# Feed-forward layers: separate semaphores for quarter loads, operand sums by copies and adding transfers, plain convolution in PSUM

## What is computed

```python
def gated_conv_ffn(x, w_gate, w_up, conv_w, conv_b, w_down):
    g = jnp.einsum('bsd,df->bsf', x, w_gate)
    g = causal_dwconv3(g, conv_w) + conv_b
    up = jnp.einsum('bsd,df->bsf', x, w_up)
    return jnp.einsum('bsf,fd->bsd', jax.nn.silu(g) * up, w_down)
```

## Time and profile before

| what | value |
|---|---|
| three runs | 1818.08, 1818.07, 1819.58 us; median 1818.08 |
| profiled execution | 1823.57 us, of it the span of the instructions 1821.9 us |
| mean granted clock of PE | 0.987 of full |
| first feed-forward layer | 873 to 1144 us of the span; its first seventh product at 922.2 |
| second feed-forward layer | 1418 to 1689 us; its first seventh product at 1466.6 |

### The profile page before, as it was taken

One profiled execution on the slowest core, in us unless ns is written; L12 is line 12 of the kernel. 1 busy time (PEld: TensorE's weight loads), 2 busy tenths in 40 slices (PEclk: granted clock), 3 DMA queues, 4 the chain that ended last, 5 costly groups with the idle time before them and its releaser, 6 DMA issues.

```text
span 1821.9 us, 29445 instructions
## 1 busy us (share of the span) xinstructions
PE 1719.3 (94%) x9907; PEld 1494.8 (82%) x9907; DVE 1126.7 (62%) x1967; ACT 892.1 (49%) x1677; POOL 649.6 (36%) x733
## 2 busy tenths in 40 slices
PE   7999999999999999999878889999999888889998
PEld 6788789999878888888678888888887678888887
DVE  6677767777743345754777777433355777877332
ACT  6676766666632233333355555323454455555222
POOL 3555666565410001001355665010013355665000
PEclk9999999999999999999999999999999999999999
DMA  4111123323233342233345554432332345554332
GB/s 132 50 50 54 50 59 83 83 70 82 70 92 92 92 144 76 70 98 94 92 103 135 125 129 111 136 99 88 93 93 81 92 100 128 138 130 108 107 95 87
DMA packets 294704, 173.58 MB, mean 95 GB/s; under 512 B 13807, under 2 KB 279922, under 8 KB 294610
## 3 DMA queue, kind: packets, MB, share of 16 engines
q1 hardware_dynamic: 281714, 148.69, 28.4%
q0 software_dynamic: 12704, 23.34, 7.3%
q10 hardware_dynamic: 192, 0.33, 0.1%
HBM read 147.02 MB, written 2.16 MB: 82 GB/s over the span
## 4 chain that ended last, share of the span: by engine, by line
PE 61%; DVE 16%; issue 8%; POOL 6%; ACT 5%; DMA 4%; DVEq 0%; ACTq 0%; POOLq 0%
PE ps L410 37%; PE ps L2559 8%; PE ps L1026 3%; DVE w_split L2620 3%; PE ps L3023 2%; DVE w_split L367 2%; PE ps L876 2%; DMA w_raw_b<-in_w_ffn_gate_dram 2%; DMA w_raw<-in_w_ffn_gate_dram 2%; POOL e_sum L2799 1%; POOL w_split L2620 1%; DVE tmp L1369 1%; PE ps L889 1%; DVE arena_r L1374 1%; PE ps L855 1%
## 5 line engine op out<-in xcount | busy, mean ns | idle before, releaser
L410 PE MATMUL ps<-arena_r,w_split 128*128 128x512 f32 x2094 | 486.3, 393 | 15.7 <-DVE w_split L367 13.9
L410 PEld LDWEIGHTS ps<-arena_r,w_split 128*128 128x128 f32 x2094 | 394.8, 189 | 104.4 <-DVE w_split L367 17.2
L410 PE MATMUL ps<-u,w_split 128*128 128x512 f32 x1641 | 400.0, 395 | 0.0
L367 DVE TENSOR_TENSOR w_split<-w_raw,w_split 128x1024 fp32r<-128x1024 f32 x149 | 188.9, 1268 | 297.1 <-ACT w_split L351 297.0
L351 ACT CAST w_split<-w_raw 128x1024 fp32r<-128x1024 f32 (+4 forms) x249 | 213.2, 874 | 300.4 <-PE ps L410 264.8
L410 PEld LDWEIGHTS ps<-u,w_split 128*128 128x128 f32 x1641 | 304.0, 188 | 62.9 <-issue 0.5
L2559 PE MATMUL ps<-xs_u,w_split 128*128 128x256 f32 x1728 | 235.8, 291 | 55.8 <-POOL w_split L2620 47.5
L2559 PEld LDWEIGHTS ps<-xs_u,w_split 128*128 128x128 f32 x1728 | 219.1, 195 | 65.3 <-DVE tmp L2915 31.6
L1977 POOL TENSOR_TENSOR tmp<-tmp 128x512 f32<-128x512 f32 x33 | 46.7, 1416 | 261.1 <-ACT tmp L1933 232.4
L365 POOL TENSOR_TENSOR w_split<-w_raw,w_split 128x256 fp32r<-128x256 f32 x168 | 123.0, 763 | 23.7 <-ACT w_split L351 23.7
L1974 POOL COPY tmp<-tmp 128x512 f32<-128x512 f32 x5 | 3.2, 649 | 349.0 <-ACT tmp L1933 183.4
(11 more groups left out here) (335 smaller groups left out, 2675.0 us busy)
## 6 DMA issues: line engine op xcount, KB each, us to landing
w_raw<-in_w_in_dram SPq DMA_DIRECT2D x118, 256.0 KB, 3.1
w_raw<-in_w_ffn_down_dram SPq DMA_DIRECT2D x64, 256.0 KB, 3.0
w_raw<-in_w_ffn_gate_dram SPq DMA_DIRECT2D x52, 256.0 KB, 3.2
w_raw<-in_w_ffn_up_dram SPq DMA_DIRECT2D x52, 256.0 KB, 3.2
w_raw_b<-in_w_ffn_up_dram SPq DMA_DIRECT2D x36, 256.0 KB, 3.2
w_raw_b<-in_w_ffn_gate_dram SPq DMA_DIRECT2D x36, 256.0 KB, 3.2
w_raw_b<-w_raw_b POOLq DMA_DIRECT2D x36, 256.0 KB, 4.3
w_raw<-w_raw POOLq DMA_DIRECT2D x36, 256.0 KB, 3.7
```

The source lines that it names most:

```text
L367: ins = eng.tensor_tensor(lo, r, hi, ALU.subtract)
L410: last = pe.matmul(out_ap, w_tile(c, ws, k - n0), moving(k, ms), start=start and n == 0, stop=stop and n == len(total) - 1, skip_group_che ...
```

## The change

- **Loads.** u1 and u2 add to a semaphore `up_load`, g1 to `g1_load`, g2 to `g2_load`, and each user waits for what it reads. The first sum waits for u1 and u2; the third sum now waits for g1.
- **Operand sums.** ACT begins the four sums by copies, with sign, of one term each (`act_x_begin`); five transfers on POOL's queue that add (`pool_x_add`, 512 KB each) complete them: T1N (one), T4 (two), T2 (one, which reads T1N), T3 (one). T4 is now begun as -B21 and gets B22 and T1N. The fifth, T3's, is issued only when T1N and T2 have landed. `pool_x` goes.
- **Plain pairs.** Their convolution, silu input and hidden rows lie in PSUM (`plain_conv`, banks 4 and 5) instead of `cnv` and `hid`. p1 of the first two pairs of the seven products waits for the low half of the plain pair that used its bank.
- **Plain units.** Units 2 to 7 all use `product_low_last`, where only unit 2 did.
- **Orders.** The written orders of ACT, DVE and POOL are changed: high and low halves of units stand earlier, POOL's first sum stands between the adding transfers.

```diff
@@ -71,6 +71,7 @@
...
 WEIGHT_OF = {"p1": "g1", "p2": "g2", "p3": "g2", "p4": "u2", "p5": "e", "p6": "g1", "p7": "u1"}
+LOADS = {"u1": "up", "u2": "up", "g1": "g1", "g2": "g2"}
 QUARTERS = ("g1", "u1", "u2", "g2")
...
@@ -245,7 +246,7 @@
...
         cnv, at = view(tmp, at, 2, SEQ)
-        hid, at = view(tmp, at, 1, SEQ)
+        at += SEQ
         rbc_ffn, at = view(tmp, at, 1, SEQ)
...
@@ -2463,8 +2464,10 @@
...
 
-        def loaded(eng, layer, i, gs):
-            eng.wait_ge(sem(f"pair_load{gs % 2}"), num(64 * (N_PAIR // 2 * layer + (gs - PLAIN) // 2 + 1), i, 128))
+        def loaded(eng, layer, i, gs, part):
+
+            per = 32 if part == "up" else 16
+            eng.wait_ge(sem(f"{part}_load{gs % 2}"), num(per * (N_PAIR // 2 * layer + (gs - PLAIN) // 2 + 1), i, 2 * per))
 
...
@@ -2504,7 +2507,7 @@
...
                 sp.dma_start(quarter(layer, gs, name).rearrange("p (k n) -> p k n", k=4), src) \
-                    .then_inc(sem(f"pair_load{gs % 2}"), 16)
+                    .then_inc(sem(f"{LOADS[name]}_load{gs % 2}"), 16)
 
...
@@ -2538,7 +2541,9 @@
...
                 out_ = bank(R_BANK + gs % 2, 0, HT)
-                if not (isinstance(i, int) and gs < PLAIN + 2):
+                if isinstance(i, int) and gs < PLAIN + 2:
+                    pe.wait_ge(sem("ffn_a_lo"), FT * layer + gs - 1)
+                else:
                     pe.wait_ge(sem("ffn_a_done"), per_tile(layer, i, gs, 2))
...
@@ -2569,19 +2574,18 @@
...
             for j in range(2 * PLAIN):
-                if j == 2:
-                    pe.wait_ge(sem("w_hi"), c0 + 3)
-                    product_low_last(pe, bank(2), c0 + 2, moving, range(KT), True, lambda: w_ready(pe, c0 + 2), True) \
-                        .then_inc(sem("w_used"), 1)
-                    continue
-                w_ready(pe, c0 + j)
-                if j < 2:
-                    pe.wait_ge(sem("h_tile"), hs_before(tag) + KT - 1 + j)
                 if j >= 4:
...
                         pe.wait_ge(sem("ffn_g_read"), PLAIN * layer + j // 2 - 1)
+                if j >= 2:
+                    pe.wait_ge(sem("w_hi"), c0 + j + 1)
+                    product_low_last(pe, bank(j % 4), c0 + j, moving, range(KT), True, lambda: w_ready(pe, c0 + j), True) \
+                        .then_inc(sem("w_used"), 1)
+                    continue
+                w_ready(pe, c0 + j)
+                pe.wait_ge(sem("h_tile"), hs_before(tag) + KT - 1 + j)
                 product(pe, bank(j % 4), c0 + j, moving, ready=h_ready(pe, tag) if j == 0 else None) \
...
@@ -2599,7 +2603,7 @@
...
             if kind in ("p1", "p2", "p4"):
-                loaded(act, layer, i, gs)
+                loaded(act, layer, i, gs, LOADS[WEIGHT_OF[kind]])
             else:
...
@@ -2624,21 +2628,30 @@
...
         X_SOURCE = {"p1": B11, "p2": B21, "p3": B22, "p4": T4, "p5": T1N, "p6": T2, "p7": T3}
-        X_SUMMED = {"p5": 1, "p6": 2, "p7": 3, "p4": 4}
+        X_SUMMED = {"p5": 1, "p6": 2, "p7": 3}
+        X_BEGUN = 4
 
...
 
-            if kind in X_SUMMED:
-                act.wait_ge(sem("x_sum"), 4 * layer + X_SUMMED[kind])
+            if kind == "p4":
+                act.wait_ge(sem("x_fourth"), 32 * layer + 32)
+            elif kind in X_SUMMED:
+                act.wait_ge(sem("x_sum"), 48 * layer + 16 * X_SUMMED[kind])
             else:
...
 
+        def act_x_begin(act, layer, m):
+
+            act.wait_ge(sem("x_dve"), X_STEPS * layer + KT)
+            dst, first, sign = ((T1N, B12, -1.0), (T4, B21, -1.0), (T2, B22, 1.0), (T3, B12, -1.0))[m]
+            act.activation(dst, first, ACT.Copy, scale=sign).then_inc(sem("x_hi"), 1)
+
         def dve_x(dve, layer, kind):
 
-            dve.wait_ge(sem("x_hi"), len(X_ORDER) * layer + X_ORDER.index(kind) + 1)
+            dve.wait_ge(sem("x_hi"), (X_BEGUN + len(X_ORDER)) * layer + X_BEGUN + X_ORDER.index(kind) + 1)
             hi, lo = XS[kind][:, :, HI, :], XS[kind][:, :, LO, :]
...
@@ -2651,14 +2664,23 @@
...
 
-        def pool_x(pool, layer, m):
-
-            pool.wait_ge(sem("x_dve"), X_STEPS * layer + KT)
-            if m in (1, 3):
-                pool.wait_ge(sem("x_sum"), 4 * layer + m)
-            dst, in0, in1, op = ((T1N, B11, B12, ALU.subtract), (T2, T1N, B22, ALU.add), (T3, B22, B12, ALU.subtract),
-                                 (T4, T2, B21, ALU.subtract))[m]
-            pool.tensor_tensor(dst, in0, in1, op).then_inc(sem("x_sum"), 1)
+        def pool_x_add(pool, layer, m):
+
+            begun = (X_BEGUN + len(X_ORDER)) * layer
+            pool.wait_ge(sem("x_hi"), begun + (1, 2, 3, 2, 4)[m])
+            if m == 2:
+                pool.wait_ge(sem("x_sum"), 48 * layer + 16)
+            elif m == 3:
+                pool.wait_ge(sem("x_sum"), 48 * layer + 16)
+                pool.wait_ge(sem("x_fourth"), 32 * layer + 16)
+            elif m == 4:
+                pool.wait_ge(sem("x_sum"), 48 * layer + 32)
+            dst, term = ((T1N, B11), (T4, B22), (T2, T1N), (T4, T1N), (T3, B22))[m]
+            pool.dma_start(dst, term, accum_op=ALU.add).then_inc(sem("x_fourth" if m in (1, 3) else "x_sum"), 16)
+
+        def plain_conv(f):
+
+            return bank(R_BANK + f % 2)
 
...
@@ -2667,20 +2689,22 @@
...
             act_stats(act, tag)
+
             def tap(f):
...
                 if f > 1:
-                    act.wait_ge(sem("ffn_a_done"), FT * layer + f - 1)
-                act.activation(cnv[:, f % 2, :], gpad[:, f % 2, 0:SEQ], ACT.Copy, scale=ffn_vec(layer, 0, f)) \
+                    act.wait_ge(sem("ffn_a_lo"), FT * layer + f - 1)
+                act.activation(plain_conv(f), gpad[:, f % 2, 0:SEQ], ACT.Copy, scale=ffn_vec(layer, 0, f)) \
                     .then_inc(sem("ffn_tap"), 1)
...
                 act.wait_ge(sem("ffn_conv"), 2 * FT * layer + 2 * f + 2)
-                act.activation(cnv[:, f % 2, :], cnv[:, f % 2, :], ACT.Silu, bias=ffn_vec(layer, 3, f)).then_inc(sem("ffn_silu"), 1)
+                act.activation(cnv[:, f % 2, :], plain_conv(f), ACT.Silu, bias=ffn_vec(layer, 3, f)) \
+                    .then_inc(sem("ffn_silu"), 1)
 
...
                 act.wait_ge(sem("ffn_a_done"), FT * layer + f + 1)
-                act.copy(a_r[:, f, HI, :], hid[:, 0, :]).then_inc(sem("ffn_a_hi"), 1)
+                act.copy(a_r[:, f, HI, :], plain_conv(f)).then_inc(sem("ffn_a_hi"), 1)
 
...
@@ -2688,29 +2712,33 @@
...
             tap(0)
+            plain_unit(3)
             silu(0)
-            plain_unit(3)
+            plain_unit(4)
+            act_x_begin(act, layer, 0)
             plain_hi(0)
-            plain_unit(4)
+            tap(1)
+            act_x_begin(act, layer, 1)
+            plain_unit(5)
+            silu(1)
+            act_x_begin(act, layer, 2)
+            act_x_begin(act, layer, 3)
             act_x(act, layer, "p1")
-            tap(1)
-            silu(1)
             act_x(act, layer, "p2")
-            plain_unit(5)
+            plain_unit(6)
+            plain_hi(1)
+            tap(2)
             act_x(act, layer, "p5")
-            plain_hi(1)
-            plain_unit(6)
-            tap(2)
             silu(2)
+            plain_unit(7)
             act_x(act, layer, "p6")
-            plain_unit(7)
+            plain_hi(2)
+            act_seventh(act, layer, 0, *ORDER[0])
             act_x(act, layer, "p7")
-            plain_hi(2)
-            act_x(act, layer, "p4")
-            act_seventh(act, layer, 0, *ORDER[0])
             tap(3)
...
             silu(3)
+            act_x(act, layer, "p4")
             act_seventh(act, layer, 0, *ORDER[2])
...
@@ -2792,7 +2820,7 @@
...
             def first_sum(i, gs):
-                loaded(pool, layer, i, gs)
+                loaded(pool, layer, i, gs, "up")
                 if not (isinstance(i, int) and gs < PLAIN + 2):
...
@@ -2800,6 +2828,7 @@
...
             def third_sum(i, gs):
+                loaded(pool, layer, i, gs, "g1")
                 pool.wait_ge(sem("summed_w"), summed_to(layer, i, gs, 1))
...
@@ -2817,14 +2846,15 @@
...
             scaled(0)
-            pool_x(pool, layer, 0)
-            pool_x(pool, layer, 1)
+            pool_x_add(pool, layer, 0)
+            pool_x_add(pool, layer, 1)
             scaled(1)
-            pool_x(pool, layer, 2)
-            pool_x(pool, layer, 3)
+            first_sum(0, PLAIN)
+            pool_x_add(pool, layer, 2)
+            pool_x_add(pool, layer, 3)
+            third_sum(0, PLAIN)
+            pool_x_add(pool, layer, 4)
             scaled(2)
-            first_sum(0, PLAIN)
-            third_sum(0, PLAIN)
             second_sum(0, PLAIN)
...
@@ -2863,44 +2893,44 @@
...
                 dve.wait_ge(sem("w_used"), c0 + 2 * f + 2)
-                if f:
-                    dve.wait_ge(sem("ffn_a_lo"), FT * layer + f)
-                dve.tensor_tensor(hid[:, 0, :], bank(2 * (f % 2) + 1), cnv[:, f % 2, :], ALU.mult).then_inc(sem("ffn_a_done"), 1)
```

(34 more changed lines are left out.)

## The result

The changed kernel takes 1794.37 us, the median of 3 runs (1793.38 to 1794.91), against 1818.08 before. The ratio is 0.9866, 95% interval 0.9844 to 0.9888: 23.7 us faster. The forecast was 1785, range 1766 to 1804. The sign and the range hold. The forecast's own case (1776 to 1795) holds by 0.6 us only, and the sum was 33.

The account below looks back on a forecast made before the run. TensorE was taken as nearly always busy, its waits mostly for GpSimd's low split in a loop through the loads. 23 us (periods) plus 10 (layer starts) gave 33 off 1818.1, so 1785, range 1766 to 1804.

Parts of the forecast that it names:

- The forecast's own case: Whole kernel: the time falls between 1776 and 1795 us, with 1785 likeliest; chance 0.49.
- Part 1: Settled periods: separate load semaphores start the first sum earlier, 0.75 us in each of 31 periods, 23 us (12 to 40).
- Rival three: Settled periods: another member of the loop holds GpSimd's round, so only 10 us are won, 1808; chance 0.11.
- Rival one: Settled periods: u2 lands as fast as g2 and takes the port first, 50 us won, 1768; chance 0.12.
- Part 2: Layer start: low-half pass last from unit 2 on, no pauses before units 3, 5, 7; plain units end 8.8 us earlier.
- Part 3: Layer start: adding transfers replace GpSimd's operand sums, p6 5.3 us earlier; after a clock loss, 10 us for two layers.
- d: Layer start: time a 512 KB adding transfer needs, taken as 6 us, between 4.9 and 8.8.
- u2 lands about 900.5: Layer start: landing time of the pair's second up load, after which GpSimd's first sum and T2's transfer follow by 902.3.
- rival four: Layer start: adding transfers held in GpSimd's queue beside full unit loads make it slower, 1830 at 17 us each; chance 0.08.
- Rival two: Layer start: its gain is eaten by slow adding transfers, only the semaphores win, 1795 or 1800; chance 0.2.
- Half a fall: Layer start: clock loss after pauses of about 3 us, set at 1.2 us and taken off the gain.
- Part 4: Layer start: plain convolution in PSUM; p1 newly waits for plain pair 2's low half, some 0.7 us, nothing else.

Follow-up runs that it names:

- e3: The changed kernel with GpSimd's wait for g1 put ahead of the first sum instead of the third; ratio 0.9842 to the kernel before.
- e1: The kernel before with the separate load semaphores and nothing else; 1800.14 us against 1820.27, ratio 0.9887.
- e2: The changed kernel with one semaphore for all four loads again; 1818.85 us, ratio 0.9991 to the kernel before.
- e11: The changed kernel with a pair's loads issued u1, u2, g1, g2 instead of u1, g1, u2, g2; ratio 0.9840 to the kernel before.
- e4: The changed kernel with GpSimd's T2 and T4 transfer issues ahead of the pair's first sum; ratio 0.9854 to the kernel before.
- e7: The changed kernel with the four operand sums computed by GpSimd again instead of adding transfers; ratio 0.9827 to the kernel before.
- e5: The changed kernel with plain pair 2's scaling ahead of GpSimd's first sum and p6's and p7's x halves later; ratio 0.9826 to the kernel before.

## Why the prediction was right, and where it was wrong

The mechanism of the periods was right and that of the starts was wrong. 1794 lies inside the range because the starts, forecast at 10 us, brought a small loss and no more, and because the periods brought somewhat more than forecast; the second of these is partly luck.

**Part 1, the semaphores: right in kind, near in number by two errors against each other.** Forecast 0.75 a period and 23 us; measured 26.8. In the settled period it was 0.52 (11.86 to 11.34: 1043.62 and 1055.48 before, 1042.14 and 1053.48 after), and 31 times that is only 16. The start of the sum came 0.75 earlier, where the prediction put it, by the split of p6, but the second wait on GpSimd took 0.26 back, which the prediction had at nothing; e3 shows that the gap is its price. The rest came from what the sum had left out. The waits of before that stand between the first pair and the layer's end, layers 1 and 2 together, are 49.1 us, those of after 30.3: 18.8 from pauses. The remaining 8.0 is clock: before had five rounds like the earlier trace rows in these two stretches, with products of up to 2.72; after has none. Not all of it hangs on the semaphores. With them alone (e1) the periods gain 19.1, and with all but them (e2) 3.3, none of it in pauses (50.3 against 49.1). The remaining 4.4 come only with both; why is not shown, and the runs of one kernel lie up to 7 us apart. Rival three (the loop holds) falls with e1. Rival one (u2 in 3.0, the port first) falls too: u2 took 3.7, and e11 shows that an earlier u2 meets DVE's split in most rounds. Its two rounds with the sum in front, at pauses of 0.24 and 0.28, are what that rival had described.

In e11 the first sum took 1.65 instead of 1.29 where DVE's split had begun 0.20 before it, and the split took 1.82 instead of 0.69 where the sum had begun 0.01 before it. By the rule of the Trainium skill (SBUF — State Buffer, Who interferes with whom), which the prediction cited, one of the two waits for the other; the rows agree.

**Part 2, plain units: right.** No pause, full clock, and 5.44 a unit instead of the 5.7 that was used. The plain units end 10.1 us earlier, from +48.80 to +38.7, where 8.8 was said.

**Part 3, the operand sums: wrong, by the loads and not by d.** Forecast: p6 5.3 earlier; measured: 0.9 later (+56.62 against +55.68). (The 19 us that it names for d = 4.9 are 17.6 by its own terms, 2 x (6.6 + 2.2).) Step by step, from the layer's start (forecast, measured): unit 7's load let go +21.07, +20.90; u2 landed +27.07, +32.1; T2 issued +28.87, +34.09; T3 landed +40.87, +46.3; p6 +50.37, +56.62. The step that failed is "u2 lands about 900.5". It allowed 6.0 us from the release for five issues and a landing, in the 0.37 and 3.8 of a settled period. It took 4.5 to reach u2's issue, with 1.45 and 1.53 for the issues of u1 and g1, and 6.7 to land. That is 5 of the 6.2 us missed; most of the rest, 0.8, is the chain from T3's landing to p6. d itself was 5.1 for T2 and 6.6 for T3, 11.7 for both where 2 x 6 was set. The prediction asked what the loads do to the adding transfers (rival four), and never what these do to the loads. e4 and e7 show that: T2 issued earlier makes u2 4.4 later; without the adding transfers u2 lands 3.8 sooner behind the release. Rival two, the start eaten, is what happened, by another route than a d near 8.8. Its number, 1795, is also nearer to the measured 1794 than the forecast is.

The Trainium skill's figure (DMA: Bandwidth & Descriptors, Anatomy of one DMA) would have made d 3.2, an estimate; the shortest here took 5.1, so the measurement decides against it. The same page (SWDGE vs HWDGE vs iDMA) says that transfers issued by GpSimd and by SP run on the same engines, and the trace agrees, with 38.8% and 67.9% of them taken at once: that rule, not weighed in the prediction, spoke against the step that failed.

**The clock in the start: too small.** Half a fall (1.2) was set. p1, p2 and the two products from p6 on took 2.90, 2.93 and 4.62, 4.2 more than at full clock. Part of it hides in the waits of p2 and p6; the 1.6 behind p6 cannot.

**Part 4, the new wait of p1: "some 0.7" was 7.98.** The prediction priced the instruction and not the queue in which its source stands. It named plain pair 2's scaling as standing behind T2's landing, and did not carry that on to p1. Nor did it see the second way to the same wait, the low half of p6's data ahead of the hidden row in DVE's queue; e5 moves both at once, and how much each holds alone was not tried. e5 shows the wait (p1 at +38.50 without it), and that it was not the only one: taking it away alone leaves 3.2 to 4.0 us per layer, since p6 is held next, by T3.

**The sum:** 26.8 - 1.6 = 25.3 in the traces, 23.7 between the medians, instead of 33. The starts' forecast of +10 against -1.6 is 11.6 of error, against which Part 1 erred by 4 the other way. Of the signs that the prediction named, the pauses (0.85 for 0.7), the period (11.34 for 11.1), GpSimd's wait for up loads and the plain units at full clock came. The first seventh product at 914 did not: it started at 916.19, in a layer that had begun 3.9 earlier. Nor did a pause of 2.5 to 3.5 before p2 for T3: p2 paused 1.21, for its own weights, and T3 showed before p6 (2.92).

## What to carry to other kernels

One semaphore for several loads makes every reader wait for the last of them; splitting it was worth 20 us of this kernel's 1820 by itself, and the one further wait that it put into GpSimd's chain cost 0.26 us a round. When work is moved from an engine to transfers, price what the transfers do to the loads that are in flight there, not just how long they take themselves. And when a new wait is added, follow its source back through the queue in which it stands until something is reached that is ready in time.

## What the runs showed that was not expected

- A second semaphore wait before a GpSimd instruction showed as 0.26 us: the gap is 0.56 with it and 0.30 without, in after and in e3.
- Beside adding transfers of 512 KB, quarter loads of 256 KB took 6.6 to 7.2 us to land instead of 3.0 to 3.8, and SP's issue of one 1.45 to 1.76 us instead of 0.37. Without these transfers (e7) it was 4.8 to 5.2, and 0.51 to 0.86.
- With T2 issued 9.6 us earlier, among the loads (e4), it took 9.0 instead of 5.1 to land.
- After 7.98 us of pause the clock stood at 0.50 for some 4 us of sparse work; after e5's pause of 11.11 two products took 5.42 instead of 3.03. These long pauses cost more than their length.
